# Hosting 30 of 36 modulation groups in three FFNs, with VectorE multiplying and adding their k-chunks

## The chip, the cores and the metric

One core of a Trainium2 chip runs the whole program in one launch. The metric is the time of one execution on the device in microseconds (us), lower is better. All data is float32. Five engines take part, each with its own in-order instruction stream: TensorE (PE in the profile, PEld for its weight loads), VectorE (DVE), ScalarE (ACT), GpSimd (POOL) and SyncE (SP), which here only issues the DMAs that load weights. They meet through semaphores: `wait_ge(sem, n)` holds an engine's stream, `then_inc(sem, n)` counts up when an instruction has finished.

## The reference

Two transformer layers over 256 latent and 256 context tokens of width 1024, then one more mixing block with an expert layer. What matters here is the modulation. Each of the two layers has nine shift, scale and gate vectors of 1024 columns, for the latent and for the context tokens, from two condition vectors:

```
mod_l = (jax.nn.silu(c) @ ada_w[i] + ada_b[i])[:, None, :]
mod_c = jax.nn.silu(c_ctx) @ ada_w[i] + ada_b[i]
sh1, sc1, g1, sh2, sc2, g2, sh3, sc3, g3 = jnp.split(mod_l, N_MOD, axis=-1)
x = ffn_step(x, sh1, sc1, g1, pre_wi, pre_wo)     # t + 0.5 * g * swiglu(modulate(rms(t), sh, sc), wi, wo)
```

`ada_w[i]` is 1024 x 9216, so a layer's modulation is a product of two rows with a large matrix: much data, little arithmetic. Each layer has an FFN before its mixer and one after it (`wi` to twice 2816 columns, `silu(g) * u`, `wo` back to 1024), and an attention between them (differential attention in the first, windowed grouped attention in the second).

## The kernel before

**Weights as a stream.** All weights lie in `w_stream` as tiles of 128 partitions x 1024 columns (512 KB). SP fetches them in order into the four slots of `raw`. ScalarE copies a slot to `w_hi` (float32r, the high part), VectorE writes `w_lo = raw - w_hi` (`split`, L1208), and TensorE makes each product in three passes (L1998 to L2000: `w_hi`*hi, `w_hi`*lo, `w_lo`*hi), 24 matmuls for a tile. `tile_used`, `lo_ready`, `hi_ready` and `raw_loaded` count tiles and hand the slots round; splits run `AHEAD = 3` tiles ahead of TensorE.

**An FFN's first half** (`ffn`, stages wi0 to wi3) takes 11 iterations of four tiles q = 0 to 3 in banks 0 to 3, a gate tile and an up tile twice. VectorE's stream for half an iteration (jj = 0, 1; L1354 to L1369): two splits, the multiplication `stage_y` (L1364), which waits until TensorE has done product q = 1 or q = 3, then `act_lo` (L1367). In the first iteration the products q = 0 to 2 are made chunk by chunk while the norm before is still being finished, and q = 3 follows.

**The modulation** is cut into 36 groups of 512 columns; a group has 4 tiles, each with two k-chunks of 128 rows. TensorE multiplies a tile's chunk by the two condition columns (L2015, `strips`): a 128x32 stationary operand `cs`, in which the two columns stand at the group's place, and 512 moving columns; the chunks go to four 32-row strips of one PSUM bank. When a batch of groups is in the bank, ScalarE copies it out (`batch_out`), TensorE turns it and sums the strips with `strip_sum` (`batch_turn`, L2022), and VectorE adds `ada_b` into `mod` (`batch_store`). Four groups are done at the start. The others are hosted: 10 in wi0 and 3 in wi1 (`side_product`, half a group after q = 0 and half after q = 2, tiles in `ada_side`, two slots, freed by `side_used`), 11 in attention A (`pair_a`) and 8 in attention B (`pair_b`), there as tiles of the `raw` ring, half a group in an attention unit (`ada_product`).

**The attentions** go through units (pair of heads, block of 128 queries), 32 in A and 16 in B. For a unit: scores on TensorE (L2268, L2356), maxima on VectorE (L1464, L1574), exponentials on ScalarE (L870, L944), weighing on VectorE (L1477, L1593), transposes on TensorE (L2279, L2368), copies on ScalarE (L882, L962); after all units of a head, values on TensorE (L2292, L2387). All of it is written out by hand in each engine's order. In B, values of head p+1 wait for `low(p)` on VectorE (L1599), which stands after the weighing of a later unit.

**Order of the loads.** SP's one queue holds tile loads and side loads; a load whose slot is not free holds back all behind it. In wi0 and wi1 `load_side` stands before tiles s = 0 and s = 2 of the next iteration, and the first one of a stage waits until the norm is done. wi1 hosts from its second iteration (`SIDE_AT`).

Of the kernel before, what the change touches and what calls it, by code (L numbers as in the profile page):

```python
# [28 lines left out]
ALU = mybir.AluOpType  # L29
AX_X = mybir.AxisListType.X  # L30

P = 128
D = 1024
KC = D // P
NT = 256
# [15 lines left out]
ADA_PART = (14, 14, 8)  # L51
# [62 lines left out]
def ring_plan():  # L114

    at, first = 0, {}
    for name, n in (("wi0", 2 * FC), ("wo0", KC * WO_T), ("qkv_a", 24),
                    ("pair_a", ADA_TILES * len(HOSTED["pair_a"])), ("out_a", KC),
                    ("wi1", 2 * FC), ("wo1", KC * WO_T), ("wi2", 2 * FC), ("wo2", KC * WO_T),
                    ("qkv_b", 12), ("pair_b", ADA_TILES * len(HOSTED["pair_b"])), ("out_b", KC),  # L120
                    ("wi3", 2 * FC), ("wo3", KC * WO_T),
                    ("proj_c", 24), ("out_c", KC), ("peer_q", PEER_ROWS), ("peer", 2 * EXPERT_CHUNKS)):
        assert at % R == 0 and n % R == 0
        first[name] = at
        at += n
    return first, at
# [3 lines left out]
ADA_AT = [(RING[pair], RING[pair] + ADA_TILES * len(HOSTED[pair])) for pair in ("pair_a", "pair_b")]  # L130


def is_ada(t):
    return any(lo <= t < hi for lo, hi in ADA_AT)


def split_at(t):

    return t - sum(max(0, min(t, hi) - lo) for lo, hi in ADA_AT)
# [8 lines left out]
def program(nc, w_stream, x_in, mem_in, small_in, const_in, rope_in, fan_in, mask_in, bias_in, sub_in, gelu_dram, out):  # L148
    with ExitStack() as ctx:
# [57 lines left out]
        ada_side = sb("ada_side", [P, 2, D], scratch + 4 * KB)  # L207
        mem_squares = sb("mem_squares", [P, KC, NT], arena + 80 * KB)
# [12 lines left out]
        o_root = sb("o_root", [P, KC, 4], scratch + 35 * KB + 512)  # L221

# [45 lines left out]
        side_used = sem("side_used")  # L268
# [209 lines left out]
        def after_ada(pair):  # L478

            return {"pair_a": [RING["out_a"] + n for n in range(AHEAD)],  # L480
                    "pair_b": [RING["out_b"] + n for n in range(AHEAD)]}.get(pair, [])
# [5 lines left out]
        def ada_first(g):  # L487

            pair = "pair_a" if g in HOSTED["pair_a"] else "pair_b"
            return RING[pair] + ADA_TILES * (g - HOSTED[pair][0])  # L490

        STRIPS = {"wi0": bank[4], "pair_a": bank[5], "wi1": bank[4], "pair_b": bank[7]}

        def batch_rows(host):

            return stage_z[:, 0, :] if host[:2] == "wi" else ada_rows[:, :]
# [16 lines left out]
        def side_used_before(f):  # L513

            return ADA_TILES * sum(hosts(n) for n in range(f))

        def wi_steps(engine, f, step, unrolled=False):


            n, last, lead = hosts(f), FC // 2, SIDE_AT.get(f"wi{f}", 0)  # L520
            for i in range(lead):
                step(i, None, False)
            step(lead, 0 if n else None, False)
            if n > 1 and unrolled:
                for i in range(1, n):
                    step(i + lead, i, False)
            elif n > 1:
                with engine.Fori(1, n) as i:
                    step(i + lead, i, False)
            rest = lead + 1  # L530
            if n:
                step(n + lead, None, True)
                rest = n + lead + 1
# [22 lines left out]
        def _(sp):  # L556
# [31 lines left out]
            def load_side(f, j, half):  # L588

                groups = HOSTED[f"wi{f}"]  # L590
                used = side_used_before(f) + 2 * half
                if isinstance(j, int) and j == 0 and half == 0:
                    sp.wait_ge(hl_ready, norm_done("pre0" if f == 0 else "post0"))
                if not (isinstance(j, int) and used + ADA_TILES * j == 0):
                    sp.wait_ge(side_used, used + ADA_TILES * j)
# [21 lines left out]
            for stage in stages:  # L617
# [3 lines left out]
                if f is not None:  # L621
                    side, lead = hosts(f), SIDE_AT.get(f"wi{f}", 0)
                    for i in range(0 if f else 1, 1 + lead):
                        load_wi(f, i, None)
                    rest = 1 + lead
                    if side:
                        load_wi(f, rest, 0)
                        with sp.Fori(1, side) as i:
                            load_wi(f, i + 1 + lead, i)
# [19 lines left out]
        def _(act):  # L649
# [19 lines left out]
            def batch_out(host):  # L669

                if host[:2] == "wi":
                    act.wait_ge(side_used, side_used_before(int(host[2:]) + 1))
# [118 lines left out]
            def ffn(f, halves, update):  # L791
# [8 lines left out]
                def chunks(i, side, done):  # L800
                    if done:
                        batch_out(f"wi{f}")
                    for jj in range(2):
                        t = t0 + 2 * jj
                        split(t + AHEAD, i, 4)
                        act.wait_ge(tile_used, t + 1 + 4 * i)
# [385 lines left out]
        def _(dve):  # L1192
# [157 lines left out]
            def ffn(f, layer, which, halves, up):  # L1350
                w = width(halves)
                t0, t1 = RING[f"wi{f}"], RING[f"wo{f}"]

                def chunks(i, side, done):  # L1354
                    for jj in range(2):
                        t = t0 + 2 * jj
                        j = FC * f + 2 * i + jj
                        if done and jj == 1:
# [20 lines left out]

                wi_steps(dve, f, chunks)  # L1380
# [5 lines left out]
                if f == 1:  # L1386
                    adjust(1, (4,), ()).then_inc(mod_ready, 1)
                    dve.wait_ge(mod_ready, 5)
                rows_out(f"wo{f}", up, lambda m, half: mod_col(layer, which, m, half), WO_T)
# [230 lines left out]
            nc.vector.memset(cs[:, :, :], 0.0)  # L1620
            link(nc.vector.memset(tiny[:, :], 0.0))
# [94 lines left out]
            adjust(0, (7,), (8,))  # L1716
            adjust(1, (1,), (2,)).then_inc(mod_ready, 1)
# [13 lines left out]
            dve.wait_ge(mod_stored, BATCH["pair_b"] + 1)  # L1731
            adjust(1, (7,), (8,)).then_inc(mod_ready, 1)
            dve.wait_ge(mod_ready, 6)
# [260 lines left out]
        def _(pe):  # L1994
# [45 lines left out]
            def side_product(f, j, half):  # L2040

                groups_before = side_used_before(f) // ADA_TILES
                for k in range(2):
                    pe.wait_ge(side_loaded[k], 16 * (2 * groups_before + half + 1) + 32 * j)
                for k in range(2):
                    strips(STRIPS[f"wi{f}"], 2 * half + k, ada_side[:, k, :], j, j == 0).then_inc(side_used, 1)
# [85 lines left out]
            def ffn(f, name, halves, update):  # L2132
                w = width(halves)
                t0, t1 = RING[f"wi{f}"], RING[f"wo{f}"]
                def steps(i, side, done):
                    if isinstance(i, int) and i == 0:
# [10 lines left out]
                        if side is not None:  # L2147
                            side_product(f, side, 0)
                        product(bank[AHEAD], t0 + AHEAD, halves)
                        if side is not None:  # L2150
                            side_product(f, side, 1)
# [511 lines left out]
```

## Time and profile before

| what | value |
|---|---|
| time, median of 3 runs | 2889.88 us (2888.32 to 2891.16) |
| span of the profiled execution | 2891.1 us, 46534 instructions |
| mean granted TensorE clock | 0.987 of full |
| PE busy | 2783.5 us (96%) |
| DVE busy | 1673.6 us (58%) |
| ACT busy | 1204.2 us (42%) |
| DMA | 445.18 MB, mean 154 GB/s |

The profile gives the profiled execution its span, from the first to the last instruction; no other time stands beside it for that execution. The span lies 1.2 us above the median. Busy time counts an instruction from start to end, and neighbours overlap a little. A timeline row has start, duration, engine, line, operation, output<-inputs, shapes and count; in brackets stands how long the engine was idle before it and what ended the wait. Start-to-start distances are what an engine's stream costs.

### The profile page before, as it was taken

To read this page: it belongs to the slowest core of one execution; us is meant where nothing else is said; L and a number is where in the kernel's file an instruction comes from. 1 tells how busy PE (TensorE), PEld (TensorE's weight loads), DVE (VectorE), ACT (ScalarE), POOL (GpSimd) and SP (SyncE) were. 2 spreads that over 40 slices of the span, in tenths; PEclk is the share of its full clock that TensorE was granted. 3 is DMA by queue.
4 is the path that set the end of the run, shared out by engine and by line. 5 is a ranking of instruction groups with operands and counts; after the bars stand their busy time and mean duration, and the time that the engine had idled before them with its cause. 6 is when DMAs were issued, how large, how long until landed. Compare 5 with 4: busy or idle time off the path is not lost.

```text
span 2891.1 us, 46534 instructions
## 1 busy us (share of the span) xinstructions
PE 2783.5 (96%) x16342; PEld 2347.9 (81%) x16342; DVE 1673.6 (58%) x2875; ACT 1204.2 (42%) x1953; POOL 164.6 (6%) x126
## 2 busy tenths in 40 slices
PE   6999999999999999999998999998999999999999
PEld 4777887756878888888885699985899999788888
DVE  5333338856633335333358665686598777677765
ACT  4222224345422324223234554456444555455444
POOL 0000003200100001000021010000060000000000
PEclk9999999999999999999999999998999999999999
DMA  7544332254342332232333645651466555677764
GB/s 277 181 175 168 102 108 68 80 209 156 113 157 95 102 103 94 95 102 92 106 101 137 211 157 181 222 164 37 154 222 197 173 175 176 210 240 241 242 200 138
DMA packets 144836, 445.18 MB, mean 154 GB/s; under 512 B 16080, under 2 KB 44880, under 8 KB 144208
## 3 DMA queue, kind: packets, MB, share of 16 engines
q1 hardware_dynamic: 112896, 409.51, 42.9%
q10 hardware_dynamic: 31824, 34.09, 3.4%
q8 instruction: 77, 1.26, 0.2%
q14 instruction: 39, 0.32, 0.0%
HBM read 428.33 MB, written 15.20 MB: 153 GB/s over the span
## 4 chain that ended last, share of the span: by engine, by line
PE 87%; DVE 7%; ACT 2%; issue 1%; DMA 1%; POOL 1%; SPq 1%; ACTq 0%; DVEq 0%; POOLq 0%
PE bank L1998 22%; PE bank L2000 22%; PE bank L1999 22%; PE bank L2521 12%; PE bank L2493 2%; PE bank L2015 2%; DVE w_lo L1208 1%; PE bank L2387 1%; PE bank L2292 1%; PE bank L2226 1%; DVE stage_rs L1409 1%; ACT w_hi L667 1%; DMA ada_start<-w_stream_dram 1%; PE bank L2368 1%; PE bank L2239 1%
## 5 line engine op out<-in xcount | busy, mean ns | idle before, releaser
L1998 PE MATMUL bank<-H,w_hi 128*128 128x256 f32 (+1 forms) x3344 | 1107.7, 331 | 22.9 <-DVE H L1244 10.6
L1208 DVE TENSOR_TENSOR w_lo<-raw,w_hi 128x1024 fp32r<-128x1024 f32 x605 | 740.1, 1225 | 634.9 <-ACT w_hi L667 627.7
L2000 PE MATMUL bank<-H,w_lo 128*128 128x256 f32 (+1 forms) x3344 | 1081.3, 323 | 0.0
L1999 PE MATMUL bank<-H,w_hi 128*128 128x256 f32 (+1 forms) x3344 | 1081.1, 323 | 0.0
L667 ACT ACTIVATE w_hi<-raw 128x1024 fp32r<-128x1024 f32 x628 | 660.2, 1052 | 233.4 <-PE bank L2000 191.0
L1998 PEld LDWEIGHTS bank<-H,w_hi 128*128 128x128 f32 x3344 | 640.3, 191 | 106.0 <-issue 44.2
L1999 PEld LDWEIGHTS bank<-H,w_hi 128*128 128x128 f32 x3344 | 640.9, 192 | 52.6 <-issue 4.8
L2000 PEld LDWEIGHTS bank<-H,w_lo 128*128 128x128 f32 x3344 | 640.0, 191 | 49.2
L1998 PE MATMUL bank<-act_hi,w_hi 128*128 128x512 f32 (+1 forms) x770 | 267.4, 347 | 0.0
L2000 PE MATMUL bank<-act_hi,w_lo 128*128 128x512 f32 (+1 forms) x770 | 266.9, 347 | 0.0
L1999 PE MATMUL bank<-act_lo,w_hi 128*128 128x512 f32 (+1 forms) x770 | 266.9, 347 | 0.0
L811 ACT ACTIVATE act_hi<-stage_y 128x512 f32 (+3 forms) x88 | 50.9, 578 | 367.4 <-DVE stage_y L1364 367.4
L1364 DVE TENSOR_TENSOR stage_y<-stage_raw,bank 128x512 f32<-128x512 f32 (+1 forms) x88 | 54.6, 620 | 190.6 <-PE bank L2000 190.6
L1999 PEld LDWEIGHTS bank<-act_lo,w_hi 128*128 128x128 f32 x770 | 145.8, 189 | 18.4
L1998 PEld LDWEIGHTS bank<-act_hi,w_hi 128*128 128x128 f32 x770 | 145.8, 189 | 18.1
L2000 PEld LDWEIGHTS bank<-act_hi,w_lo 128*128 128x128 f32 x770 | 145.8, 189 | 17.9
L2521 PE MATMUL bank<-w_hi,pw_hi 128*128 128x512 f32 x512 | 158.1, 390 | 2.0 <-DVE pw_lo L1869 2.0
L2521 PE MATMUL bank<-w_lo,pw_hi 128*128 128x512 f32 x512 | 157.8, 389 | 0.0
L2521 PE MATMUL bank<-w_hi,pw_lo 128*128 128x512 f32 x512 | 157.6, 389 | 0.0
L807 ACT ACTIVATE stage_raw<-bank 128x512 f32<-128x512 f32 (+1 forms) x88 | 47.7, 542 | 198.0 <-PE bank L2000 198.0
L1138 ACT ACTIVATE pw_hi<-pw 128x256 fp32r<-128x256 f32 x128 | 53.4, 417 | 179.9 <-PE bank L2521 145.4
L2521 PEld LDWEIGHTS bank<-w_lo,pw_hi 128*128 128x128 f32 x512 | 96.1, 188 | 20.3
(239 smaller groups left out, 2458.7 us busy)
## 6 DMA issues: line engine op xcount, KB each, us to landing
raw<-w_stream_dram SPq DMA_DIRECT2D x704, 512.0 KB, 3.4
ada_side<-w_stream_dram SPq DMA_DIRECT2D x52, 512.0 KB, 4.2
gelu_scratch<-gelu ACTq DMA_DIRECT2D x108, 128.0 KB, 3.7
gelu_in<-gelu_scratch ACTq DMA_DIRECT2D x108, 128.0 KB, 3.5
ada_start<-w_stream_dram SPq DMA_DIRECT2D x16, 512.0 KB, 13.9
bias<-bias_in_dram ACTq DMA_DIRECT2D x1, 3072.0 KB, 10.3
X<-x_in_dram SPq DMA_DIRECT2D x1, 2048.0 KB, 10.5
mem<-mem_in_dram SPq DMA_DIRECT2D x1, 1024.0 KB, 6.4
```

What stands on the lines that cost most here:

```text
L667: nc.scalar.activation(w_hi[:, s, :], raw[:, s, :], ACT.Copy).then_inc(hi_ready, 1)
L807: nc.scalar.activation(stage_raw[:, jj, 0:w], bank[2 * jj][:, 0:w], ACT.Silu).then_inc(silu_done, 1)
L811: nc.scalar.activation(act_hi[:, 2 * i + jj, 0:w], stage_y[:, jj, 0:w], ACT.Copy).then_inc(act_hi_ready, 1)
L1138: nc.scalar.activation(pw_hi[:, b, :], pw[:, b, :], ACT.Copy).then_inc(of("peer", "w_hi"), 1)
L1208: nc.vector.tensor_tensor(w_lo[:, s, :], raw[:, s, :], w_hi[:, s, :].bitcast(F32), ALU.subtract).then_inc(lo_ready, 1)
L1364: nc.vector.tensor_tensor(stage_y[:, jj, 0:w], stage_raw[:, jj, 0:w], bank[2 * jj + 1][:, 0:w], ALU.mult).then_inc(a_ready, 1)
L1998: nc.tensor.matmul(to, w_hi[:, s, cut], hi, start=first, stop=False, skip_group_check=True)
L1999: nc.tensor.matmul(to, w_hi[:, s, cut], lo, start=False, stop=False, skip_group_check=True)
L2000: return nc.tensor.matmul(to, w_lo[:, s, cut], hi, start=False, stop=last, skip_group_check=True)
L2015: ins = nc.tensor.matmul(to[at:at + STRIP, :], cs[:, 2 * n + k, C_AT - 2 * row:C_AT - 2 * row + STRIP], tile[:, k * 512:(k + 1) * 512], st ...
L2493: ins = nc.tensor.matmul(bank[q][:, n * P:(n + 1) * P], spread2[:, q % 2, n, :], spread1[:, q % 2, n, :], start=True, stop=True)
L2521: ins = nc.tensor.matmul(bank[2 * half + dh][:, :], weights[:, b, toks], tile[:, t % R, dh * 512:(dh + 1) * 512], start=False, stop=True, ...
```

## The change

Attention B hosts nothing, attention A hosts 2 groups instead of 11, wi0 still 10, wi1 10 instead of 3, and wi2 10 instead of none. The way in which an FFN hosts a group is new. VectorE multiplies each k-chunk by its condition column and adds it to `part`, two rows of 512 columns per partition (one for each condition vector): 2 `tensor_scalar` and 14 `scalar_tensor_tensor` of 128x512 for a group, one quarter (a tile) after each `stage_y` and each `act_lo`. TensorE then makes only the sum over partitions: `side_sum`, four matmuls of 256 columns with a column of ones (`row_pick`) at the group's place. It stands after product q = 0 of the iteration that follows the group's. `side_added` counts VectorE's adds (16 for a group), `part_summed` TensorE's sums; `load_side` waits for the adds of the slots it refills, and stands after tiles s = 1 and s = 3. The bank of the strips is set to zero before the stage. Which columns are adjusted where (`adjust`) follows the new places of the groups. After attention B the three first splits of `out_b` are now made in `project("qkv_b")`, since no tiles lie between.

```diff
-ADA_HOST = (("wi0", 10), ("pair_a", 11), ("wi1", 3), ("pair_b", 8))
+ADA_HOST = (("wi0", 10), ("pair_a", 2), ("wi1", 10), ("wi2", 10))
-SIDE_AT = {"wi0": 0, "wi1": 1}
-BATCH_MAX = 11
+BATCH_MAX = 10
+SIDE_ADDS = 4 * ADA_TILES
...
+        part = sb("part", [P, 2, 512], scratch + 16 * KB)
+        row_pick = sb("row_pick", [P, 2 * BATCH_MAX - 1 + STRIP], scratch + 35 * KB + 640)
...
                 for s in range(R):
-                    if side is not None and s % 2 == 0:
+                    load_tile(f"wi{f}", s, i)
+                    if side is not None and s % 2 == 1:
                         load_side(f, side, s // 2)
-                    load_tile(f"wi{f}", s, i)
...
+                def side_tile(j, n):
+                    before = groups_before(f)
+                    dve.wait_ge(side_loaded[n % 2], 16 * (2 * before + n // 2 + 1) + 32 * j)
+                    for k in range(2):
+                        for v in range(2):
+                            add = 4 * n + 2 * k + v
+                            src, scale = ada_side[:, n % 2, k * 512:(k + 1) * 512], cs[:, 2 * n + k, C_AT + v:C_AT + v + 1]
+                            if add >= 2:
+                                dve.wait_ge(side_added, SIDE_ADDS * before + add - 1 + SIDE_ADDS * j)
+                                ins = nc.vector.scalar_tensor_tensor(out=part[:, v, :], in0=src, scalar=scale,
+                                                                     in1=part[:, v, :], op0=ALU.mult, op1=ALU.add)
+                            else:
+                                if not (isinstance(j, int) and before + j == 0):
+                                    dve.wait_ge(part_summed, before + j)
+                                ins = nc.vector.tensor_scalar(part[:, v, :], src, scale, None, ALU.mult)
+                            ins.then_inc(side_added, 1)
...
                         nc.vector.tensor_tensor(stage_y[:, jj, 0:w], stage_raw[:, jj, 0:w], bank[2 * jj + 1][:, 0:w],
                                                 ALU.mult).then_inc(a_ready, 1)
+                        if side is not None:
+                            side_tile(side, 2 * jj)
                         dve.wait_ge(act_hi_ready, j + 1)
                         nc.vector.tensor_tensor(act_lo[:, 2 * i + jj, 0:w], stage_y[:, jj, 0:w],
                                                 act_hi[:, 2 * i + jj, 0:w].bitcast(F32), ALU.subtract
                                                 ).then_inc(act_lo_ready, 1)
+                        if side is not None:
+                            side_tile(side, 2 * jj + 1)
...
+            def side_sum(f, j):
+                to, first = STRIPS[f"wi{f}"], 2 * BATCH_MAX - 1
+                pe.wait_ge(side_added, SIDE_ADDS * (groups_before(f) + j + 1))
+                for v in range(2):
+                    for half in range(2):
+                        at, cut = STRIP * (2 * v + half), slice(half * NT, (half + 1) * NT)
+                        ins = nc.tensor.matmul(to[at:at + STRIP, cut], row_pick[:, first - 2 * j - v:first - 2 * j - v + STRIP],
+                                               part[:, v, cut], start=j == 0, stop=j == hosts(f) - 1, skip_group_check=True)
+                ins.then_inc(part_summed, 1)
...
                     for q in range(4):
                         product(bank[q], t0 + q, halves, i, 4)
+                        if q == 0 and hosts(f) and isinstance(i, int) and i <= hosts(f):
+                            side_sum(f, i - 1)
                         if q == 1 and done:
                             batch_turn(f"wi{f}")
-                        if side is not None and q % 2 == 0:
-                            side_product(f, side, q // 2)
```

## Rows read from the trace of the kernel before

**Rows 1.** The page: busy times and the chain's shares by engine.

```profile
PE 2783.5 (96%) x16342; PEld 2347.9 (81%) x16342; DVE 1673.6 (58%) x2875; ACT 1204.2 (42%) x1953; POOL 164.6 (6%) x126
...
PE 87%; DVE 7%; ACT 2%; issue 1%; DMA 1%; POOL 1%; SPq 1%; ACTq 0%; DVEq 0%; POOLq 0%
```

**Rows 2.** Stretches: length, PE, PEld, DVE, ACT, POOL busy, clock, DMA share, GB/s.

```profile
60.00:75.00 15.00, 13.86 (x68) 9.58 (x67) 7.44 (x11) 7.62 (x11) 0.00 (x0) 1.00 0.81 282
...
1636.00:1645.00 9.00, 6.28 (x40) 6.31 (x41) 6.28 (x9) 7.12 (x9) 0.00 (x0) 0.80 0.56 189
...
1961.00:1990.00 29.00, 22.87 (x156) 12.38 (x155) 19.40 (x92) 22.16 (x83) 0.00 (x0) 1.00 0.01 1
```

**Rows 3.** Timeline of PE in wi0, around a half group.

```profile
91.14 0.39 PE L1998 MATMUL bank<-H,w_hi 128*128 128x512 f32 x1
...
96.68 1.07 PE L2015 MATMUL bank<-ada_side,cs 128*32 128x512 f32 x8
97.67 0.50 PE L1998 MATMUL bank<-H,w_hi 128*128 128x512 f32 x1
```

**Rows 4.** Timeline of VectorE, `stage_y` in wi0 (hosted).

```profile
91.42 0.69 DVE L1364 TENSOR_TENSOR stage_y<-stage_raw,bank 128x512 f32<-128x512 f32 x1 [3.94 <-PE bank L2000]
...
115.63 0.69 DVE L1364 TENSOR_TENSOR stage_y<-stage_raw,bank 128x512 f32<-128x512 f32 x1 [3.94 <-PE bank L2000]
```

**Rows 5.** Timeline of VectorE, `stage_y` in wi1, across the batch and after.

```profile
857.85 0.69 DVE L1364 TENSOR_TENSOR stage_y<-stage_raw,bank 128x512 f32<-128x512 f32 x1 [2.71 <-PE bank L2000]
...
880.49 0.69 DVE L1364 TENSOR_TENSOR stage_y<-stage_raw,bank 128x512 f32<-128x512 f32 x1 [2.63 <-PE bank L2000]
...
891.37 0.69 DVE L1364 TENSOR_TENSOR stage_y<-stage_raw,bank 128x512 f32<-128x512 f32 x1 [2.63 <-PE bank L2000]
```

**Rows 6.** VectorE's groups by form: count | busy us, mean ns.

```profile
L1208 DVE TENSOR_TENSOR w_lo<-raw,w_hi 128x1024 fp32r<-128x1024 f32 x605 | 740.1, 1225 | 634.9 <-ACT w_hi L667 627.7
L1593 DVE TENSOR_SCALAR probs<-probs,tiny 128x512 f32<-128x512 f32 x32 | 14.1, 484 | 0.6
L1477 DVE SCALAR_TENSOR_TENSOR probs<-probs,tiny 128x512 f32<-128x512 f32 x16 | 12.0, 752 | 0.6
```

**Rows 7.** Timeline of VectorE, attention A.

```profile
623.56 0.75 DVE L1477 SCALAR_TENSOR_TENSOR probs<-probs,tiny 128x512 f32<-128x512 f32 x1
624.23 0.75 DVE L1464 TENSOR_REDUCE tiny<-bank 128x1 f32<-128x256 f32 x2
```

**Rows 8.** `ada_side` in 100:300, issue to landing.

```profile
DMA to landing us min/median/max: 3.2/4.2/5.2
```

**Rows 9.** Timeline of VectorE at the start of wi1.

```profile
769.78 0.68 DVE L1364 TENSOR_TENSOR stage_y<-stage_raw,bank 128x512 f32<-128x512 f32 x1
...
774.68 0.68 DVE L1364 TENSOR_TENSOR stage_y<-stage_raw,bank 128x512 f32<-128x512 f32 x1
```

**Rows 10.** Timeline of PE, values in attention A.

```profile
658.05 2.94 PE L2292 MATMUL bank<-V,pT 128*128 128x128 f32 x24
...
669.40 2.94 PE L2292 MATMUL bank<-V,pT 128*128 128x128 f32 x24
...
680.15 2.94 PE L2292 MATMUL bank<-V,pT 128*128 128x128 f32 x24
```

**Rows 11.** Timeline of all engines, one head of attention B.

```profile
1579.26 1.13 PE L2356 MATMUL bank<-K,Q 64*128 64x512 f32 x4
...
1583.24 0.42 DVE L1599 TENSOR_TENSOR H<-bank,H 128x256 fp32r<-128x256 f32 x1
...
1583.80 1.95 PE L2387 MATMUL bank<-pT,V 128*64 128x256 f32 x16 [0.34 <-DVE H L1599]
...
1585.68 1.09 PE L2368 MATMUL bank<-consts,probs 128*128 128x128 f32 x8
...
1592.24 1.95 PE L2387 MATMUL bank<-pT,V 128*64 128x256 f32 x16 [0.34 <-DVE H L1599]
```

**Rows 12.** Timeline of PE, first product after attention B.

```profile
1638.72 0.35 PE L1998 MATMUL bank<-H,w_hi 128*128 128x256 f32 x1 [2.77 <-DVE w_lo L1208]
```

More of the change, by code:

```diff
@@ L129 @@
 RING, N_RING = ring_plan()
-ADA_AT = [(RING[pair], RING[pair] + ADA_TILES * len(HOSTED[pair])) for pair in ("pair_a", "pair_b")]
+ADA_FROM, ADA_TO = RING["pair_a"], RING["pair_a"] + ADA_TILES * len(HOSTED["pair_a"])
 def is_ada(t):
-    return any(lo <= t < hi for lo, hi in ADA_AT)
+    return ADA_FROM <= t < ADA_TO
 def split_at(t):
-    return t - sum(max(0, min(t, hi) - lo) for lo, hi in ADA_AT)
+    return t - max(0, min(t, ADA_TO) - ADA_FROM)
 def ada_source(g):
@@ L478, in after_ada @@
         def after_ada(pair):
-            return {"pair_a": [RING["out_a"] + n for n in range(AHEAD)],
-                    "pair_b": [RING["out_b"] + n for n in range(AHEAD)]}.get(pair, [])
+            return [RING["out_a"] + n for n in range(AHEAD)] if pair == "pair_a" else []
         def ada_half(u):
@@ L487, in ada_first @@
         def ada_first(g):
-            pair = "pair_a" if g in HOSTED["pair_a"] else "pair_b"
-            return RING[pair] + ADA_TILES * (g - HOSTED[pair][0])
-        STRIPS = {"wi0": bank[4], "pair_a": bank[5], "wi1": bank[4], "pair_b": bank[7]}
+            return RING["pair_a"] + ADA_TILES * (g - HOSTED["pair_a"][0])
+        STRIPS = {"wi0": bank[4], "pair_a": bank[5], "wi1": bank[4], "wi2": bank[4]}
         def batch_rows(host):
-            return stage_z[:, 0, :] if host[:2] == "wi" else ada_rows[:, :]
+            return stage_sq[:, 0, :] if host[:2] == "wi" else ada_rows[:, :]
         def selector(n):
@@ L511, in hosts, with groups_before @@
             return len(HOSTED.get(f"wi{f}", []))
-        def side_used_before(f):
-            return ADA_TILES * sum(hosts(n) for n in range(f))
+        def groups_before(f):
+            return sum(hosts(n) for n in range(f))
         def wi_steps(engine, f, step, unrolled=False):
[L520 to L523, printed above, removed]
+            n, last = hosts(f), FC // 2
+            step(0, 0 if n else None, False)
             if n > 1 and unrolled:
                 for i in range(1, n):
-                    step(i + lead, i, False)
+                    step(i, i, False)
             elif n > 1:
                 with engine.Fori(1, n) as i:
-                    step(i + lead, i, False)
-            rest = lead + 1
+                    step(i, i, False)
+            rest = 1
             if n:
-                step(n + lead, None, True)
-                rest = n + lead + 1
+                step(n, None, True)
+                rest = n + 1
             if rest < last:
@@ L590, in load_side @@
                 groups = HOSTED[f"wi{f}"]
-                used = side_used_before(f) + 2 * half
+                added = SIDE_ADDS * groups_before(f) + SIDE_ADDS // 2 * half
                 if isinstance(j, int) and j == 0 and half == 0:
-                    sp.wait_ge(hl_ready, norm_done("pre0" if f == 0 else "post0"))
-                if not (isinstance(j, int) and used + ADA_TILES * j == 0):
-                    sp.wait_ge(side_used, used + ADA_TILES * j)
+                    sp.wait_ge(hl_ready, norm_done(("pre0", "post0", "pre1")[f]))
+                if not (isinstance(j, int) and added + SIDE_ADDS * j == 0):
+                    sp.wait_ge(side_added, added + SIDE_ADDS * j)
                 for k in range(2):
@@ L621, in _ @@
                 if f is not None:
[L622 to L625, printed above, removed]
+                    side = hosts(f)
+                    if f:
+                        load_wi(f, 0, None)
+                    rest = 1
                     if side:
@@ L800, in chunks @@
                 def chunks(i, side, done):
-                    if done:
-                        batch_out(f"wi{f}")
                     for jj in range(2):
@@ L805, in chunks @@
                         split(t + AHEAD, i, 4)
+                        if done and jj == 0:
+                            batch_out(f"wi{f}")
                         act.wait_ge(tile_used, t + 1 + 4 * i)
@@ L1378, in chunks @@
                         ins.then_inc(mem_split, 1)
+                if hosts(f):
+                    nc.vector.memset(STRIPS[f"wi{f}"][:, :], 0.0)
                 wi_steps(dve, f, chunks)
```

36 lines of the change are left out of this document (14 added, 22 removed).

## The prediction

> **What bounds the kernel now.** I read the page first, then the stretches, then timelines. TensorE is busy in 96% of the span and holds 87% of the chain of waits; VectorE is busy in 58% [rows 1]. The reader is to see that the FFN stages have nothing to give but TensorE's own instructions: in wi0 TensorE runs product after product, and hosted work stands between two of them as a plain addition. From the last matmul group of a product to the next product lie 96.68 to 97.67, 0.99 us for half a group of strips [rows 3]. `stage_y` comes once in half an iteration and so measures TensorE's pace: unhosted 10.88 us (the last two of [rows 5]), so a product takes 5.44 and an iteration 21.76; hosted 24.21 [rows 4]. A hosted group costs 24.21 - 21.76 = 2.45 us in an FFN. In the attentions TensorE shares the path with VectorE and ScalarE, so a hosted half group costs less there than its 0.99.
>
> **The question that decides the sum** is not VectorE's load. An iteration takes 4 splits, 2 `stage_y`, 2 `act_lo` and then 2 `tensor_scalar` and 14 `scalar_tensor_tensor`. The trace has both of the added kinds at 128x512: 484 and 752 ns [rows 6], and the second starts its successor after 0.67 us [rows 7]. With about 1.15, 0.61, 0.61 and 0.42 for the others (their durations less the same overlap of 0.07), that is 4.6 + 1.2 + 1.2 + 0.8 + 9.4 = 17.3 us of some 24: it fits. The question is when the last add of a group is done. Its second half stands behind the `stage_y` that waits for product q = 3, and `side_sum` stands on TensorE only one product later.
>
> Let E be the start of the next iteration's product q = 0. `stage_y` starts at E + 0.28 (91.42 against 91.14) [rows 3, 4]. Then come `stage_y` 0.61, four adds 4 x 0.67 = 2.68, `act_lo` 0.61 (ScalarE makes `act_hi` during the adds, so that wait is free), three adds 2.01, the last one in full 0.75, and 0.05 to reach TensorE: E + 7.0. TensorE is through with q = 0 at E + 5.44 and **waits 1.55 us** in each hosted iteration. All of TensorE's later products are queued behind that wait, and next VectorE's `stage_y`. `side_sum` is no row of this trace: it has the count of matmuls of half a hosted group (8 in the trace) at half the columns, so between half of 0.99 and 0.99; I take 0.56, near the half, and 0.14 for the restart (half a hosted iteration costs 1.22, of which 0.99 are strips). A group then costs 7.0 + 0.56 + 0.14 - 5.44 = 2.3 us, not less than now. Bounds: 0.8 if the wait were not there, 3.0 if each add started only after the one before was done and the sum took the full 0.99.
>
> **Part by part** (profiled execution, span 2891.1).
>
> *First group of a stage.* There VectorE also comes late to `stage_y`. In wi1 the first `stage_y` starts at 769.78 and the second at 774.68 [rows 9]; between them now come `act_lo`, eight adds (2 x 0.42 + 6 x 0.67) and two splits: 769.78 + 0.61 + 0.61 + 4.9 + 2.35 = 778.3. The loads for tiles 2 and 3 start only when tile 1 is added, at 776.1, and land 4.2 later [rows 8], at 780.3. Then 2.68 + 0.61 + 2.76 + 0.05 = 786.4, where the steady rule gives 781.1: 5.2 us more. The same holds in wi2; in wi0 I take 5.0, less the 1.1 us for which TensorE idles today in 60:75 [rows 2], as its first side tiles land late. TensorE thus stands still for some 7 us three times. After 2.77 us of idle [rows 12] the granted clock is 0.80 over 9 us [rows 2], which is about 3.6 us at 1.2 GHz and 1.8 us lost; I add 3 x 1.8 = 5.4 (bounds 0 and 10).
>
> *wi0:* 10 x (2.3 - 2.45) + 5.0 - 1.1 = +2.4. *wi1:* 10 x 2.3 + 5.2 - 3 x 2.45 = +20.9. *wi2:* 10 x 2.3 + 5.2, and one batch turned, which costs 880.49 - 857.85 - 21.76 = 0.9 [rows 5]: +29.1. The bank's memset is a few tenths on VectorE, hidden in ScalarE's table load; the added `adjust` instructions are hidden under the first `wo` products; if not, a microsecond.
>
> *Attention A* loses 18 of 22 half groups. A head with three takes 669.40 - 658.05 = 11.35, the next one, with two, 680.15 - 669.40 = 10.75 [rows 10]: 0.6 each. Upper bound 0.99, TensorE's own time; I take 0.65, since without them the round through VectorE, ScalarE and TensorE binds: -12 (-10 to -18). The batch's copy, turn and store only move to an early head.
>
> *Attention B* loses all 16. A head takes 1592.24 - 1583.80 = 8.44. Its round without strips: from scores at 1579.26 to the end of `low` at 1583.66 are 4.4, then values and transposes, 1585.68 - 1583.80 = 1.88 and about 1.0 [rows 11]: 4.45 + 1.9 + 1.0 = 7.4. Only one of the two half groups lies on that round, the other beside VectorE. Seven heads x 1.04 = 7.3; the first head, in which strips run and wait for tiles, 2.3. At the end the splits of `out_b` no longer stand between the last `low` and the product: of the 2.77 us of idle [rows 12] some 1.8 go. But three splits move into `qkv_b`, where VectorE is nearly always late: 3 x 1.23 at most [rows 6], none at least; I take 2.4, as it has small waits there. Sum -9.0 (-4 to -16).
>
> *SP's queue.* In steady state the loads of tiles 2 and 3 start when tile 1 is added and have 5.3 us until `side_tile(2)` wants them, against 4.2 median and 5.2 longest landing [rows 8]; those of tiles 0 and 1 have over 6. Tile loads behind them still land before ScalarE's slot is free. Cost 0; if a landing takes longer, its excess is added to TensorE's wait one for one.
>
> *Sum:* 2.4 + 20.9 + 29.1 + 5.4 - 12 - 9.0 = +36.8. On the profiled span 2927.9; on the median, which is 1.2 lower, **2927 us**.
>
> **A rule that speaks louder against the change.** The trace's `scalar_tensor_tensor` of 128x512 reads both tensors as float32 from SBUF, as the added ones do, and starts its successor after 0.67 us [rows 7]. The Trainium skill (Vector Engine (DVE) Microarchitecture Reference, "Points that are easy to get wrong") says that such an instruction "with two non-bf16 SBUF sources halves throughput". If that came on top of the row, the adds would take 1.34, a group's chain would end near E + 12 and the kernel near 3085 us. I give this 0.02, because the row has just these operands.
>
> **The rivals.**
> - *The adds are covered by product q = 0; faster.* One place: the wait in `side_sum`. It vanishes if VectorE's chain of 2.3 + 7p us (p: distance of two adds) ends within 5.44, so for p below 0.45; the whole change breaks even near p = 0.55. Then groups cost 0.8: 30 x 0.8 + 0.9 - 24.5 - 7.4 - 1.1 - 21.0 = -29, **2861 us**. For it: `tensor_scalar` at 484 ns shows that VectorE can be faster. Against: 14 of 16 adds read two tensors and have 752 [rows 6]. 0.09.
> - *The clock falls after each wait.* 27 further losses of 1.8: +49, **2976 us**. Against: in 60:75 an idle of 1.1 us left the clock at 1.00, and attention C, with TensorE busy 22.87 of 29 us in pieces, too [rows 2]. 0.06.
> - *Side tiles land late each time,* by 1 us in steady state: +27, **2954 us**. Against: the landings of [rows 8]. 0.07.
> - *The attentions don't gain,* since something else holds them: **2948 us**. For it: VectorE and ScalarE are on their rounds too. Against: the head with one strip pair less is 0.6 us shorter [rows 10]. 0.04.
>
> **How the numbers follow.** Forecast 0.72, rivals 0.09, 0.06, 0.07, 0.04 and 0.02. The range 2906 to 2950 takes a group's cost from 2.0 to 2.7, the first groups and the clock from half to one and a half times, and the attentions from -14 to -30; it takes in the late tiles partly and the attentions' failure, and leaves out the faster case, the clock and the rule. Two thousandths are what can be told from no change. Slower by more: 0.88 (all but the first rival and the lower edge of the forecast); within: 0.03; faster: 0.09.
>
> **What would show it.** `side_sum` idles about 1.5 us before it, 30 times, released by VectorE's adds to `part`, and some 7 us the first time in each stage. `stage_y` comes 24 us after the one before last in the hosted iterations of all three stages. Heads of A take about 9.5 us, heads of B 7.4. The forecast is wrong if TensorE doesn't wait at `side_sum`, if the adds take clearly less than 0.67 us each, or if the clock is below 1.00 throughout wi0.

## The result and the profile after

| | median of 4 runs, us | range |
|---|---|---|
| before | 2890.14 | 2888.32 to 2891.16 |
| after | 2922.47 | 2919.86 to 2923.52 |
| ratio | 1.0108 | 1.0095 to 1.0120 |

The change makes the kernel 1.1% slower: +32.3 us, where 2927 us and +36.8 were forecast. The profiled execution has a span of 2919.8 against 2891.1, 28.7 more.

The page of the kernel after, busy times and the chain's shares, to be held against [rows 1]:

```profile
PE 2748.8 (94%) x16102; PEld 2345.1 (80%) x16102; DVE 1961.2 (67%) x3360; ACT 1202.9 (41%) x1953; POOL 167.4 (6%) x126
...
PE 79%; DVE 11%; issue 5%; ACT 3%; DMA 1%; POOL 1%; SPq 0%; DVEq 0%; ACTq 0%; POOLq 0%
PE bank L2023 20%; PE bank L2025 19%; PE bank L2024 19%; PE bank L2546 12%; DVE part L1363 4%; PE bank L2518 2%; DVE w_lo L1206 1%; PE bank L2412 1%; PE bank L2317 1%; PE bank L2251 1%; ACT w_hi L665 1%; DVE stage_rs L1436 1%; PE bank L2073 1%; DMA ada_start<-w_stream_dram 1%; PE bank L2393 1%
```

TensorE did lose work: 34.7 us less busy. The span grew all the same, and the chain says where: TensorE's share falls from 87% to 79%, VectorE's grows from 7% to 11%, and the only new VectorE line with a large share is the added one (L1363, 4%). "issue", time in which an engine waited for nothing that the profile shows, grows from 1% to 5%. 67% busy is far from full; load is not what the chain shows.

The groups by form of the same kernel, the lines that the change added (count | busy us, mean ns | idle before, releaser):

```profile
L1363 DVE SCALAR_TENSOR_TENSOR part<-ada_side,cs,part 128x512 f32<-128x512 f32 x420 | 288.4, 746 | 1.3 <-DMA ada_side<-w_stream_dram 1.3
L1368 DVE TENSOR_SCALAR part<-ada_side,cs 128x512 f32<-128x512 f32 x60 | 26.3, 480 | 0.0
L2073 PE MATMUL bank<-part,row_pick 128*32 128x256 f32 x240 | 20.1, 407 | 47.8 <-DVE part L1363 47.8
```

Both kinds of add cost what the trace of before had for them (752 and 484 ns) [rows 6]. In front of `side_sum` TensorE stands still for 47.8 us in all. That is where the time went, and one steady iteration shows how. First VectorE in wi1, then TensorE's sum in the same iteration (columns as in [rows 3, 4]):

```profile
795.20 0.69 DVE L1381 TENSOR_TENSOR stage_y<-stage_raw,bank 128x512 f32<-128x512 f32 x1 [2.55 <-PE bank L2025]
795.80 2.74 DVE L1363 SCALAR_TENSOR_TENSOR part<-ada_side,cs,part 128x512 f32<-128x512 f32 x4
798.45 0.69 DVE L1386 TENSOR_TENSOR act_lo<-stage_y,act_hi 128x512 f32 x1
799.05 2.74 DVE L1363 SCALAR_TENSOR_TENSOR part<-ada_side,cs,part 128x512 f32<-128x512 f32 x4
801.71 2.36 DVE L1206 TENSOR_TENSOR w_lo<-raw,w_hi 128x1024 fp32r<-128x1024 f32 x2
808.19 0.69 DVE L1381 TENSOR_TENSOR stage_y<-stage_raw,bank 128x512 f32<-128x512 f32 x1 [4.13 <-PE bank L2025]
```

```profile
800.21 0.39 PE L2025 MATMUL bank<-H,w_lo 128*128 128x512 f32 x1
801.85 0.64 PE L2073 MATMUL bank<-part,row_pick 128*32 128x256 f32 x8 [1.25 <-DVE part L1363]
802.42 0.50 PE L2023 MATMUL bank<-H,w_hi 128*128 128x512 f32 x1
```

VectorE waits for TensorE (2.55 us before this `stage_y`, 4.13 before the next), then has eight adds, an `act_lo` and nothing else until 801.79, and TensorE, done with product q = 0 at 800.60, waits for the last of the adds. Two engines wait for each other in turn, each with idle time to spare. In wi0 the steady wait is 1.31 and an iteration 23.95; in wi1 and wi2 they are 1.25 and 23.87. Four adds take 2.74, so one starts its successor after (2.74 - 0.75) / 3 = 0.66 us. The rule of the Trainium skill that was weighed (Vector Engine (DVE) Microarchitecture Reference, "Points that are easy to get wrong": such an instruction "with two non-bf16 SBUF sources halves throughput") would have had 1.34 here; the trace disagrees with it as a surcharge on the old row: these adds read two float32 tensors of SBUF and keep 746 ns and 0.66 us.

The heads of attention A (values) and of B after, against [rows 10, 11]; the last line of the first fence is A's last head:

```profile
620.03 2.94 PE L2317 MATMUL bank<-V,pT 128*128 128x128 f32 x24
629.89 2.94 PE L2317 MATMUL bank<-V,pT 128*128 128x128 f32 x24
...
679.94 5.49 PE L2317 MATMUL bank<-V,pT 128*128 128x128 f32 x24 [1.85 <-ACT pT L880]
```

```profile
1621.26 1.95 PE L2412 MATMUL bank<-pT,V 128*64 128x256 f32 x16 [1.09 <-DVE H L1626]
1628.70 1.95 PE L2412 MATMUL bank<-pT,V 128*64 128x256 f32 x16 [1.08 <-DVE H L1626]
```

The distance of two heads is now 9.86 in A, against 11.35 with three half groups, and 7.44 in B, against 8.44. Without strips TensorE waits more for the other engines: in A 7.9 us for ScalarE's `probs` and 4.8 for VectorE's over 600 to 680, against 0.2 and 3.4 over 600 to 690 before. So less is won for a half group than its own 0.99.

To place the whole difference I took the distances between landmarks that all kernels have (first `stage_y` of a stage, first matmul of `wo`, first scores, first product of `out`). Each is the difference of two starts in the timelines. wi0 is counted from the start of TensorE's sum of the squares of `mem`, its work just ahead of product q = 3: in the kernel before, wi0's first `stage_y` stood behind a split whose tile landed late, 3.83 us after that sum's start, and 1.56 after it in the new one. Counted from `stage_y`, wi0 would seem unchanged (249.33 and 249.05).

| stretch, us | before | after | difference | forecast |
|---|---|---|---|---|
| wi0 | 253.16 | 250.61 | -2.55 | +2.4, clock +1.8 |
| wi1 | 230.19 | 250.92 | +20.73 | +20.9, clock +1.8 |
| wi2 | 221.88 | 250.05 | +28.17 | +29.1, clock +1.8 |
| attention A | 100.66 | 92.55 | -8.11 | -12 |
| `wo2`, `qkv_b` and attention B | 273.44 | 265.07 | -8.37 | -9.0 with the head of `out_b` |
| `out_b` to wi3's first `stage_y` | 43.39 | 41.84 | -1.55 | 0 |
| everything else | | | +0.4 | 0 |
| sum | | | +28.7 | +36.8 |

"Everything else" is the start of the kernel (+0.9), its end (-0.6) and four differences of at most 0.1; two runs of one kernel, experiments 1 and 9, differ by 1.0 in the same start. The row of `out_b` is no such scatter: the stretch takes 41.6 to 42.1 in all ten traces with the new places. Before, the granted clock was 0.80 at its head, after the 2.77 us of idle [rows 2, 12]; now it is 1.00 there (1671 to 1676).

### The profile page after: what moved, and what is told of

Read it like the earlier page. It is cut to its first block, busy times and chain, and to the rows that moved or that the text cites. A ratio compares the mean times of both kernels' runs of the same rounds, so it can differ in the third digit from the quotient of the medians.

```text
span 2919.8 us, 46772 instructions
## 1 busy us (share of the span) xinstructions
PE 2748.8 (94%) x16102; PEld 2345.1 (80%) x16102; DVE 1961.2 (67%) x3360; ACT 1202.9 (41%) x1953; POOL 167.4 (6%) x126
## 4 chain that ended last, share of the span: by engine, by line
PE 79%; DVE 11%; issue 5%; ACT 3%; DMA 1%; POOL 1%; SPq 0%; DVEq 0%; ACTq 0%; POOLq 0%
PE bank L2023 20%; PE bank L2025 19%; PE bank L2024 19%; PE bank L2546 12%; DVE part L1363 4%; PE bank L2518 2%; DVE w_lo L1206 1%; PE bank L2412 1%; PE bank L2317 1%; PE bank L2251 1%; ACT w_hi L665 1%; DVE stage_rs L1436 1%; PE bank L2073 1%; DMA ada_start<-w_stream_dram 1%; PE bank L2393 1%
## 5 line engine op out<-in xcount | busy, mean ns | idle before, releaser
L1363 DVE SCALAR_TENSOR_TENSOR part<-ada_side,cs,part 128x512 f32<-128x512 f32 x420 | 288.4, 746 | 1.3 <-DMA ada_side<-w_stream_dram 1.3
```

The source lines that it names most:

```text
L1363: ins = nc.vector.scalar_tensor_tensor(out=part[:, v, :], in0=src, scalar=scale, in1=part[:, v, :], op0=ALU.mult, op1=ALU.add)
```

## Experiments

Every kernel was timed in turn with the kernel before on its chip (1, 2, 5 and 6 in 3 rounds, the others in 5), whose median was 2890.7 to 2891.2 each time. Ratios are to that kernel, with a 95% interval in brackets. `...` in an edit marks what is left out.

**1. Where does the wait come from: the place of the sum, or the adds?** The sum moved one product later; nothing else but what belongs to it (the batch's turn and copy) moves along.

```diff
-                        if q == 0 and hosts(f) and ...: side_sum(f, i - 1)
-                        if q == 1 and done: batch_turn(f"wi{f}")
+                        if q == 1 and hosts(f) and ...: side_sum(f, i - 1)
+                        if q == 2 and done: batch_turn(f"wi{f}")
```

> The changed kernel with side_sum one product later (after q = 1), its batch copied out in the second half iteration and turned after q = 2. Theory (TensorE stands still at side_sum because VectorE's chain ends 7 us after the iteration's end): the 47.8 us of idle ahead of side_sum in the changed kernel vanish, the low clock after the long first waits too (5 us), and about 0.1 us a group comes back as drain and restart: 2922 - 48 - 5 + 3 = 2873 us, an iteration of 22.6 us, faster than the kernel before. Rival (a hosted group costs what it costs wherever the sum stands: its matmuls, the extra weight change, VectorE's and the DMAs' traffic): 2922. Second rival (the next group's first adds then wait for the sum and make VectorE late): the wait moves to VectorE, 2890 to 2915.

Measured: 2866.94 us (2864.78 to 2867.72), 0.9916 of before [0.9900, 0.9933]. The same instructions, 55 us less than the change and 24 less than before. Its groups by form and one iteration of VectorE in wi1:

```profile
L1363 DVE SCALAR_TENSOR_TENSOR part<-ada_side,cs,part 128x512 f32<-128x512 f32 x420 | 288.5, 747 | 4.0 <-DMA ada_side<-w_stream_dram 4.0
L2073 PE MATMUL bank<-part,row_pick 128*32 128x256 f32 x240 | 19.2, 391 | 0.6 <-DVE part L1363 0.6
```

```profile
825.08 0.69 DVE L1381 TENSOR_TENSOR stage_y<-stage_raw,bank 128x512 f32<-128x512 f32 x1 [2.01 <-PE bank L2025]
...
836.76 0.69 DVE L1381 TENSOR_TENSOR stage_y<-stage_raw,bank 128x512 f32<-128x512 f32 x1 [2.64 <-PE bank L2025]
...
847.64 0.69 DVE L1381 TENSOR_TENSOR stage_y<-stage_raw,bank 128x512 f32<-128x512 f32 x1 [2.01 <-PE bank L2025]
```

The idle time before the sum falls from 47.8 to 0.6 us, an iteration from 23.87 to 847.64 - 825.08 = 22.56, and a group costs 22.56 - 21.76 = 0.80 instead of 2.11. VectorE does as much work as in the changed kernel and still idles 2.0 to 2.6 us twice per iteration. The shorter iterations are 20 x 1.31 + 10 x 1.40 (wi0) = 40 us. Some 14 more come from the first groups of the three stages and their clock (1.00 over 740 to 780), as wi0, wi1 and wi2 fall by 15.2, 19.7 and 18.8 in all. I had forecast 2873, with 0.1 us a group coming back as drain and restart. Nothing came back: 1.31 and 1.40 are a little more than the waits of 1.25 and 1.31.

**2. Half of the adds, the sum in its early place.** The context column's adds after its first are left out, so seven of sixteen, and their products are missing in the modulations.

```diff
+                            if add >= 2 and v == 1:
+                                continue
...
-                            ins.then_inc(side_added, 1)
+                            ins.then_inc(side_added, 2 if add >= 2 else 1)
```

> The changed kernel with side_sum in its place after q = 0, but of the adds for the second condition column (context) only the first one is made: 9 instructions a group instead of 16; part of the modulation is left out. Theory: VectorE's chain ends near E + 4.8, before product q = 0 does at E + 5.44, so the wait vanishes as in the run before: 2873 us. Rival (the cost is the sum's own or its place's): 2922. If the wait is only shortened by the adds' time without vanishing: 2885.

Measured: 2869.85 us (2869.63 to 2874.12), 0.9930 [0.9914, 0.9947]; 22.56 us per iteration, and 3.6 us idle before the sum in all of the kernel. In the steady iterations a shorter chain and a later sum are worth the same. It doesn't yet say whether the load or the chain's end counts; 3 and 4 do.

**3. Three early adds less.** Adds 3, 5 and 7 of a group are left out. They stand ahead of the `stage_y` of product q = 3.

```diff
+                            if add in (3, 5, 7):
+                                continue
...
```

> The changed kernel without three of a group's sixteen adds, all from its first half (tiles 0 and 1, context column), which stands ahead of the stage_y of product q = 3; those three products are missing in the modulations. Theory (only what VectorE does after that stage_y ends the wait in front of the sum): VectorE idles some 2 us more before that stage_y and nothing else moves; the wait stays 1.25 us and an iteration 23.87. Only the first group of each stage, where VectorE comes late to stage_y, gains up to 3 x 0.66 = 2: 2922.5 - 3 x 2 = 2916.5, at most 2922.5. Rival (VectorE's load is what binds, each add is worth its pitch): 30 x 3 x 0.66 = 59 us less, limited by the wait to 30 x 1.35 = 40: about 2882.

Measured: 2915.86 us (2913.02 to 2917.09), 1.0083 [1.0069, 1.0096].

**4. One late add less.** Add 13 is left out, which stands behind that `stage_y`. In both edits the counts of `side_added` are adapted so that the sum still waits for the last add.

```diff
+                            if add in (13,):
+                                continue
...
```

> The changed kernel without one of a group's sixteen adds, from its second half (tile 3, context column), which stands after that stage_y; that product is missing in the modulations. Theory: the chain ends one pitch earlier, the wait falls from 1.25 to 0.6 us and an iteration from 23.87 to 23.2; 30 x 0.66 = 20 us less: 2902.5. So one late add is worth more than three early ones. Rival (load): a third of what three early adds bring. Rival (the end of the chain isn't made of the adds but of a landing tile or of ScalarE's act_hi): 2922.

Measured: 2903.09 us (2901.84 to 2905.42), 1.0041 [1.0027, 1.0054]. The timeline of both engines in wi1, VectorE's late half and the sum: without three early adds, then without one late add.

```profile
837.49 0.69 DVE L1383 TENSOR_TENSOR stage_y<-stage_raw,bank 128x512 f32<-128x512 f32 x1 [2.64 <-PE bank L2027]
838.09 2.74 DVE L1365 SCALAR_TENSOR_TENSOR part<-ada_side,cs,part 128x512 f32<-128x512 f32 x4
840.74 0.69 DVE L1388 TENSOR_TENSOR act_lo<-stage_y,act_hi 128x512 f32 x1
841.34 2.74 DVE L1365 SCALAR_TENSOR_TENSOR part<-ada_side,cs,part 128x512 f32<-128x512 f32 x4
...
844.14 0.64 PE L2075 MATMUL bank<-part,row_pick 128*32 128x256 f32 x8 [1.25 <-DVE part L1365]
```

```profile
834.24 2.73 DVE L1365 SCALAR_TENSOR_TENSOR part<-ada_side,cs,part 128x512 f32<-128x512 f32 x4
836.89 0.68 DVE L1388 TENSOR_TENSOR act_lo<-stage_y,act_hi 128x512 f32 x1
837.50 2.20 DVE L1365 SCALAR_TENSOR_TENSOR part<-ada_side,cs,part 128x512 f32<-128x512 f32 x3
...
839.75 0.64 PE L2075 MATMUL bank<-part,row_pick 128*32 128x256 f32 x8 [0.71 <-DVE part L1365]
```

This is the clearest pair of the study. Ninety adds taken from in front of `stage_y` leave the wait at 1.25 us; of the 6.6 us that they bring, 6.2 lie at the stage starts (wi0, wi1, wi2: -1.2, -3.1, -1.9), where the first waits fall from 2.51, 5.42 and 5.56 to 1.31, 3.70 and 3.84. Thirty adds taken from behind it shorten the wait to 0.71 and the kernel by 19.4 us. Of these 15.7 lie in the three stages (-5.5, -5.6, -4.6), or 0.52 an add against 0.07 for an early one; most of the rest lies in the attentions (-1.1, -1.6), where nothing was changed, and is scatter. The load is refuted: what counts is the end of the chain that starts at the last `stage_y`.

**5. The old method in the new places.** No adds on VectorE; TensorE's strips host all 30 groups in the FFNs.

```diff
...
-                        if side is not None: side_tile(side, 2 * jj)
...
-                        if side is not None: side_tile(side, 2 * jj + 1)
...
-                if hosts(f):
-                    nc.vector.memset(STRIPS[f"wi{f}"][:, :], 0.0)
...
-                        if q == 0 and hosts(f) and ...: side_sum(f, i - 1)
+                        if side is not None and q % 2 == 0: side_product(f, side, q // 2)
```

> The groups stand where the changed kernel has them (10, 2, 10, 10), but the FFNs host them in the old way: TensorE multiplies with cs, VectorE adds nothing. Theory: 17 more groups at 2.45 in wi1 and wi2 (+41.7), one batch (+0.9), qkv_b's splits (+2), attentions -8 and -10, 2 at the end: 2890 + 25 = 2915 us; so the move out of the attentions is what costs, and the VectorE way at its place pays back nearly nothing of it. Rival (VectorE's adds are what makes the changed kernel slow, the move pays by itself): under 2890.

Measured: 2921.77 us (2920.37 to 2922.92), 1.0104 [1.0087, 1.0121]. The strips:

```profile
L2034 PE MATMUL bank<-ada_side,cs 128*32 128x512 f32 x480 | 64.5, 609 | 7.1 <-DMA ada_side<-w_stream_dram 7.1
```

So moving the groups alone, with the load order of the changed kernel, costs +31 us, and putting VectorE in the strips' place with the early sum changes +0.7 more, which the ranges of the two don't tell from nothing. An iteration is 24.21 with strips and 23.87 (wi0: 23.95) with adds and sum, which over 30 groups favours the adds by 9 us; wi0, wi1 and wi2 come out only 2.2, 0.3 and 0.6 shorter than with strips, and the other 6 us go into the first groups, where the wait for the adds is long. Outside of them the profile of the strips is 2.1 us shorter, in pieces below 1 us, the start among them. I had 2915: the 7.1 us in which strips wait for their tiles at the starts of stages (0.8, 3.3 and 2.9; 1.1 in all before) I had not expected. They are 6 of the 31 us; whether earlier loads would win them back, no run tried. The whole change is a placement at a loss, plus a method that gains nothing until its sum stands in the right place.

**6. Is attention A the cheaper place?** Nine groups in A and three in wi1, with the early sum:

```diff
-ADA_HOST = (("wi0", 10), ("pair_a", 2), ("wi1", 10), ("wi2", 10))
+ADA_HOST = (("wi0", 10), ("pair_a", 9), ("wi1", 3), ("wi2", 10))
```

> The changed kernel with 9 groups in attention A and 3 in wi1 instead of 2 and 10; all else as it is. Theory from the traces: a group in wi1 costs 2.11 (23.87 a hosted iteration against 21.76), half a group in A (11.35 - 9.86) / 3 = 0.50: -7 x 2.11 + 14 x 0.50 = -7.8, 2915 us. Rival (strips in A cost TensorE's own 0.99 each): 2921. Rival (they are free in A): 2908.

Measured: 2914.51 us (2913.12 to 2915.94), 1.0082 [1.0065, 1.0098]. wi1 falls by 15.4 us, 2.2 a group, and A grows by 5.8 against the 92.55 of the changed kernel, 0.42 for each of its 14 half groups. But that 92.55 is high: the same A takes 91.0 to 91.4 in six of the seven other traces that have it. Against these A grows by 6.9 to 7.4, about the 0.50 a half group that was expected.

**7. The same with the late sum.** The edit of 1 and the edit of 6 together.

> Hosts wi0 10, attention A 9, wi1 3, wi2 10, with the sum after the second product (q = 1) as in e1_sum_after_q1. Theory (with the late sum an FFN group costs only its sum, 22.56 - 21.76 = 0.8 us, and a group in attention A, two half groups, costs 5.8 / 7 = 0.83): moving seven groups from wi1 to A changes nothing, 2866 to 2868 us, wi1 231.2 - 7 x 0.8 = 225.6 and A 91.2 + 5.8 = 97. Rival (the attentions are still the cheaper place, as when the sum was early: 2914.5 against 2922.5): about 2859. Rival (the FFN is now the cheaper place, half groups in A cost their 0.6 to 0.65 each as I first predicted): 2867 + 7 x (1.25 - 0.8) = 2870.

Measured: 2868.76 us (2866.82 to 2871.22), 0.9924 [0.9910, 0.9937], against 2867.54 for the late sum alone on the same chip: no difference that can be told. wi1 fell by 5.7 us, 0.8 a group as expected. A grew by 10.8, from 90.97 to 101.75, where 5.8 was expected. More than 1 us of the gap comes from the 5.8, which 6 shows to be too low. Besides, in A's first head a strip waited for its tile,

```profile
588.35 1.22 PE L2040 MATMUL bank<-raw,cs 128*32 128x512 f32 x8 [1.96 <-DMA raw<-w_stream_dram]
```

and the granted clock went to 0.74 over 590 to 595. The kernel of 6 waited 0.69 us at that place and kept its clock (1.00). With the late sum the FFN is no dearer a place than A.

**8. The sum still later,** after q = 2, the turn after q = 3.

```diff
-                        if q == 0 and hosts(f) and ...: side_sum(f, i - 1)
-                        if q == 1 and done: batch_turn(f"wi{f}")
+                        if q == 2 and hosts(f) and ...: side_sum(f, i - 1)
+                        if q == 3 and done: batch_turn(f"wi{f}")
```

> As e1_sum_after_q1, but the sum stands after the third product (q = 2) and the batch is turned after the fourth. Theory (only the wait in front of the sum cost time, and it is already nil after q = 1): the same as e1, 2867 us within 2; the sum's own 0.8 us is left, an iteration 22.56. VectorE's next adds then start later, as the bank of partial sums is read later, and its idle of 2.0 to 2.6 us in front of stage_y must cover that. Rival (that slack is too small, the next group's adds and with them stage_y come late): an iteration over 23 us, over 2880. Rival (part of the gain of e1 was a clock or a start effect that a still later sum improves further): the first group of wi0, which cost 2.6 us more than those of wi1 and wi2, comes down and the time is 2864.

Measured: 2868.88 us (2865.18 to 2869.68), 0.9924 [0.9911, 0.9938]; two starts of `stage_y` in wi1 are 839.80 and 862.36, again 22.56. One row shows what the place costs elsewhere:

```profile
L1368 DVE TENSOR_SCALAR part<-ada_side,cs 128x512 f32<-128x512 f32 x60 | 26.5, 484 | 119.7 <-PE bank L2073 119.7
```

VectorE now waits 119.7 us for the sum before a group's first add, and `stage_y`, before which it idled, starts right behind its splits. The slack has been used up without loss. wi0, counted from its first `stage_y`, stays at 234.3, 3.1 more than wi1. That isn't made by the side sum, nor is it the price of a first group, as I had taken it in the forecast of this run: wi0's stretch holds the last 2 of the 3.61 us in which TensorE sums the squares of `mem`, and wi1's begins only 1.3 us into product q = 3.

**9. The late sum once more,** the kernel of 1 beside 7 and 8.

> The kernel of e1_sum_after_q1 once more, on the chip of its two neighbours and in more rounds: 2867 us, 0.9916 of the kernel before. If it were not below 0.9950, what e1 showed would be the chip's or the run's.

Measured: 2867.54 us (2864.86 to 2869.64), 0.9919 [0.9906, 0.9933]. It stands: the version with the late sum is faster than both kernels.

## Why the prediction was right, and where its terms were off

**Which question decides.** Right. I had argued that VectorE's load fits and that the end of the last add decides; 3 and 4 show it directly, and 1 by moving the reader of the adds.

**The chain, E + 7.0.** E, the start of q = 0, is 795.20 - 0.28 = 794.92; the sum starts at 801.85, at E + 6.93. The idle row says 1.25 where I had 1.55, since q = 0's last matmul ends at E + 5.68 and not at E + 5.44, which is its distance to the next product. That is a matter of the row and not of the time. The group cost 23.87 - 21.76 = 2.11 instead of 2.3: 0.07 from the chain, and 0.57 from the sum to the next product where I had 0.70 with the restart. In wi0 it is 23.95 - 21.76 = 2.19. Over 30 groups that is -4.9 us against the forecast.

**First groups.** I had 5.2 and the clock's 1.8, 7.0 together. What wi1 and wi2 show over their groups is 20.7 - 21.1 + 7.35 = 7.0 and 28.2 - 21.1 - 0.9 = 6.2, so the sum was right. Its parts were not quite: the first wait is 5.42 and 5.56, that is 4.2 and 4.3 over a steady one, and 2.8 and 1.9 are left, which I put down to the clock (0.89 around both waits). The wait was shorter because the tiles of the late half came 3.2 us after their issue (766.04 to 769.22) and not 4.2. TensorE's sum in the three stages, with the row that stands ahead of wi0's product q = 3:

```profile
55.24 3.61 PE L2173 MATMUL bank<-mem_squares,consts 128*128 128x256 f32 x16
...
72.25 0.64 PE L2073 MATMUL bank<-part,row_pick 128*32 128x256 f32 x8 [2.51 <-DVE part L1363]
...
775.26 1.08 PE L2073 MATMUL bank<-part,row_pick 128*32 128x256 f32 x8 [5.42 <-DVE part L1363]
...
1169.77 1.08 PE L2073 MATMUL bank<-part,row_pick 128*32 128x256 f32 x8 [5.56 <-DVE part L1363]
```

Here is the step that failed, wi0's 5.0. From the stage's first `stage_y` (56.80 and 759.97) to the sum are 15.45 us in wi0 and 15.29 in wi1: VectorE's chain is the same. TensorE is through with q = 0 after 12.94 in wi0 and after 9.87 in wi1, 3 us later, since in wi0 it sums the squares of `mem` (3.61 us) before product q = 3. That work was there in the kernel before, in the code and in the trace (54.39, 3.61 us), and I had not counted it as cover. The wait was 2.51 us, only 1.2 over a steady one, the clock stayed at 1.00, and wi0 came out at -2.55 instead of +4.2: 10 x (2.19 - 2.45) + 1.2 - 1.1 is -2.5. The forecast had 5.0 and 1.8 where 1.2 and nothing came. The stretches around the first waits of wi0 and wi1, and a later one (columns as in [rows 2]; the clock stands after POOL's):

```profile
60.00:90.00 30.00, 27.49 (x128) 22.09 (x127) 27.58 (x41) 10.03 (x13) 0.00 (x0) 1.00 0.50 178
765.00:795.00 30.00, 24.58 (x103) 19.15 (x101) 20.47 (x28) 6.25 (x8) 0.00 (x0) 0.89 0.52 177
795.00:1000.00 205.00, 193.76 (x898) 154.81 (x897) 147.19 (x205) 53.69 (x69) 0.00 (x0) 1.00 0.49 177
```

**Attention A.** The mis-sized term: -8.1 instead of -12. A head takes 9.86 instead of 11.35, 0.50 for a half group, not 0.65. I had generalised from the one step from three half groups to two (0.60 [rows 10]). Eighteen times 0.50 are 9.0; 1.0 came back in the last head, whose values took 5.49 us at a granted clock of 0.72 (680 to 690) where before they took 4.50. That last part is scatter: the same A takes 91.0 to 91.4 in six other traces, 9.2 to 9.7 less than before, so the term was some 2.5 too large.

**Attention B.** Right: 1628.70 - 1621.26 = 7.44 a head against 7.4. The moved splits cost 2.0 against 2.4: they are all that changed in `qkv_b`, which grew from 195.46 to 197.43 with `wo2`'s end. One gain was left out of the sum: I had taken the low clock after the 2.77 us of idle as the price of a stall, but not counted that with this idle gone `out_b` gets it back, 1.55 us.

**The rivals.** "Adds covered" needed p below 0.45 and measured 0.66. "The clock falls after each wait" is refuted by the 205 us at 1.00 with nine waits of 1.25 in them. "Late tiles" is refuted as a steady cost: all adds together waited 1.3 us for DMA. "The attentions don't gain" is refuted: they gave 16.5 us.

**Net,** measured less forecast, on the profile: the groups -4.9, wi0's first group with its clock -5.6, wi2's -0.8, `out_b`'s clock -1.55, the rest +0.4; A +3.9, B +0.6; together -8.0. The errors in part cancel, so some of the closeness is luck: the mechanism of the steady wait was right to 0.2 us a group, wi0's first group was not. The median grew by 32.3, 3.6 more than the profiled span did, so it is only 4.5 us under the forecast.

## What to carry to other kernels

When work moves to an engine with idle time, its load says only whether it fits; work out when its *last* instruction is done, counted from the last event that the engine itself has to wait for, and put the consumer behind that. Here one product of distance turned +1.1% into -0.8% with the same instructions. And try placement and method apart: the places alone, with their load order, had cost +31 us, which the method had to earn back first.

## What the runs showed of the hardware

- Adds that alternate between two accumulators follow each other after 0.66 us; adds that use the same accumulator twice in a row, where the program makes the second wait on `side_added` until the first is done, after 1.60 - 0.75 = 0.85. The row is of the kernel with half the adds, two adds to one accumulator; the same effect is why the late add left out in 4 saved 0.54 us of wait and not 0.66:

```profile
841.78 1.60 DVE L1365 SCALAR_TENSOR_TENSOR part<-ada_side,cs,part 128x512 f32<-128x512 f32 x2
```

- Stalls of TensorE of 1.24 to 1.32 us, one in each hosted iteration, left the granted clock at 1.00 (90 to 305, 795 to 1000, 1178 to 1380), and the one of 2.51 did too; those of 5.42 and 5.56 were accompanied by 0.89 over 765 to 795 and over 1160 to 1190 (from 2.4 to 1.2 GHz for part of it), and those of 3.70 and 3.84 in experiment 3 by 0.94 over 760 to 790 and 1152 to 1182. The length of the stall alone doesn't decide: in attention A of experiment 7 one of 1.96, with TensorE busy for only 2.30 of the 5 us from 585 on, was followed by 0.74 over 5 us.
